# State-space scan: decay sums and their exponentials kept as DRAM rows and read back to all partitions, in place of selector and mask products

## The reference, cut to what matters

```
cum = cumsum(a_c)                            # a = dt * A, along the 128 tokens
seg = cum[i] - cum[j]
decay = exp(where(i >= j, seg, -inf))        # 128 x 128 for each head
cb = C_c @ B_c.T                             # one for a group of 4 heads
y_intra = (cb * decay) @ x_c
y_inter = (C_c @ state) * exp(cum)
new_state = state * exp(cum[-1]) + B_c.T @ (exp(cum[-1] - cum) * x_c)
```

## Time and profile before

| what | value |
|---|---|
| time, median of 3 runs | 1479.23 us (1479.05 to 1479.36) |
| span of the profiled execution | 1476.2 us |
| its own time beside the span | not listed apart; the median of the runs lies 3.0 us above the span |
| PE busy | 98% of the span |
| DVE, ACT, POOL busy | 60%, 42%, 13% |
| PE on the chain of work that ended last | 91% |
| DMA moved | 142.9 MB, mean 97 GB/s |

### The profile page before, as it was taken

One profiled execution on the slowest core, in us unless ns is written; L12 is line 12 of the kernel. 1 busy time (PEld: TensorE's weight loads), 2 busy tenths in 40 slices (PEclk: granted clock), 3 DMA queues, 4 the chain that ended last, 5 costly groups with the idle time before them and its releaser, 6 DMA issues.

```text
span 1476.2 us, 25723 instructions
## 1 busy us (share of the span) xinstructions
PE 1451.7 (98%) x10269; PEld 1154.9 (78%) x10269; DVE 883.7 (60%) x1223; ACT 622.1 (42%) x965; POOL 197.0 (13%) x233
## 2 busy tenths in 40 slices
PE   8999999999999999999999999999999999999897
PEld 4778788787888888788887888888887777777676
DVE  3677677777545765964546443244334876666736
ACT  4664444454555523232334432134323444453534
POOL 0000000000027888820005100000000000000000
PEclk9999999999999999999999999999999999999999
DMA  9432222223245666532332333333332311211111
GB/s 318 130 86 72 72 73 74 79 63 83 75 128 145 167 174 173 169 101 86 100 101 73 100 100 101 100 86 100 100 100 72 86 45 45 60 44 42 51 42 57
DMA packets 263980, 142.89 MB, mean 97 GB/s; under 512 B 4869, under 2 KB 261946, under 8 KB 263866
## 3 DMA queue, kind: packets, MB, share of 16 engines
q1 hardware_dynamic: 263866, 141.26, 33.6%
HBM read 139.14 MB, written 2.10 MB: 96 GB/s over the span
## 4 chain that ended last, share of the span: by engine, by line
PE 91%; DVE 4%; ACT 2%; SPq 1%; issue 1%; DMA 1%; DVEq 0%; ACTq 0%
PE PS L594 25%; PE PS L596 24%; PE PS L595 24%; PE PS L815 1%; PE PS L799 1%; PE PS L1088 1%; PE PS L1104 1%; DMA wm<-in_w_mod_dram 1%; DVE Hl L1860 1%; PE PS L779 1%; PE PS L820 1%; SPq L413 1%; PE PS L1096 1%; PE PS L1044 1%; PE PS L985 1%
## 5 line engine op out<-in xcount | busy, mean ns | idle before, releaser
L594 PE MATMUL PS<-Hh,whi 128*128 128x512 f32 x1226 | 502.7, 410 | 2.7 <-DVE Hl L1860 2.3
L596 PE MATMUL PS<-Hh,wlo 128*128 128x512 f32 x1226 | 478.8, 391 | 0.0
L595 PE MATMUL PS<-Hl,whi 128*128 128x512 f32 x1226 | 478.7, 390 | 0.0
L1848 DVE TENSOR_TENSOR wlo<-raw,whi 128x1024 fp32r<-128x1024 f32 (+1 forms) x211 | 283.4, 1343 | 113.5 <-ACT whi L1283 112.7
L1283 ACT ACTIVATE whi<-raw 128x1024 fp32r<-128x1024 f32 (+1 forms) x211 | 221.7, 1051 | 151.5 <-PE PS L596 146.5
L594 PEld LDWEIGHTS PS<-Hh,whi 128*128 128x128 f32 x1226 | 230.5, 188 | 65.9 <-issue 19.4
L596 PEld LDWEIGHTS PS<-Hh,wlo 128*128 128x128 f32 x1226 | 230.6, 188 | 50.0 <-issue 0.2
L595 PEld LDWEIGHTS PS<-Hl,whi 128*128 128x128 f32 x1226 | 231.1, 188 | 46.5 <-issue 4.8
L492 POOL TENSOR_TENSOR mbuf<-mbuf,cact 128x1024 f32<-128x1024 f32 x32 | 62.2, 1944 | 438.8 <-DMA mbuf<-in_w_mod_dram 438.8
L594 PE MATMUL PS<-YBh,whi 128*128 128x512 f32 x256 | 99.6, 389 | 0.0
L595 PE MATMUL PS<-YBl,whi 128*128 128x512 f32 x256 | 99.6, 389 | 0.0
(11 more groups left out here) (426 smaller groups left out, 1822.3 us busy)
## 6 DMA issues: line engine op xcount, KB each, us to landing
raw<-in_w_in_dram SPq DMA_DIRECT2D x106, 512.0 KB, 4.0
raw<-in_w_ff_dram SPq DMA_DIRECT2D x64, 512.0 KB, 4.1
mbuf<-in_w_mod_dram SPq DMA_DIRECT2D x32, 512.0 KB, 3.9
wm<-in_w_mod_dram SPq DMA_DIRECT2D x8, 1024.0 KB, 10.8
raw<-in_w_branch_ssm_dram SPq DMA_DIRECT2D x16, 512.0 KB, 4.0
raw<-in_w_out_dram SPq DMA_DIRECT2D x10, 512.0 KB, 4.1
raw<-in_w_branch_gm_dram SPq DMA_DIRECT2D x8, 512.0 KB, 4.1
raw<-in_w_out_dram SPq DMA_DIRECT2D x6, 448.0 KB, 3.9
```

What stands on the lines that cost most here:

```text
L594: pe.matmul(bank[:, :], whi[s][:, k, :], xh[:, kk, :], start=kk == 0, stop=False)
L595: pe.matmul(bank[:, :], whi[s][:, k, :], xl[:, kk, :], start=False, stop=False)
L596: last = pe.matmul(bank[:, :], wlo[s][:, k, :], xh[:, kk, :], start=False, stop=t == end - 1 and k == (order or range(kt))[-1])
L1848: v.tensor_tensor(wlo[s][:, 0:kt, :], raw[s][:, 0:kt, :], whi[s][:, 0:kt, :].bitcast(F32), ALU.subtract).then_inc(s_wlo, 1)
```

## The change

The kernel after computes the sums once as fp32 rows on 32 partitions (`er`: sums, `et`: their exponentials). SP writes both to DRAM (`rows_out`), waits for them, and for each chunk issues a transfer that reads one row of 4 heads x 128 tokens back to all 128 partitions (`load_rows`: `crow`, and for c > 0 `erow`), two buffers of each. The mask and selector products, their constants, and the splitting into bf16 parts go. ACT makes Relu(own sum - row) for four heads and one Exp over 512 columns with scale -1; DVE multiplies the 128 x 128 block C B with `triu` (in `inputs`) in place of the mask, and `receivers` reads `erow` in place of bank 6.

```diff
+    erow = region(60, *((f"erow{i}", [P, T]) for i in range(2)))
+    cum_rows, exp_rows = (nc.dram_tensor(name, (NC, 32 * P), F32, kind="Internal").ap() for name in ("cum_rows", "exp_rows"))
...
+        def rows_out():
+            sp.wait_ge(s_dta, 8)
+            for to, rows in ((cum_rows, er), (exp_rows, et)):
+                sp.dma_start(to.rearrange("c (h t) -> h c t", t=P),
+                             rows[0:32, :].rearrange("p (c t) -> p c t", c=NC)).then_inc(s_rows, 16)
+            sp.wait_ge(s_rows, 32)
+
+        def load_rows(n):
+            g, c = divmod(n, NC)
+            e = 3 * g + c - 1
+            at = slice(g * T, (g + 1) * T)
+            if n >= 2:
+                sp.wait_ge(s_dec, n - 1)
+            sp.dma_start(crow[n % 2][:, :], cum_rows[c:c + 1, at].to_broadcast([P, T])).then_inc(s_crow[n % 2], 16)
+            if c > 0:
+                if e >= 2:
+                    sp.wait_ge(s_ch, e - 1)
+                sp.dma_start(erow[e % 2][:, :], exp_rows[c:c + 1, at].to_broadcast([P, T])).then_inc(s_erow[e % 2], 16)
+
+        rows_after = {}
+        for n in range(30):
+            g, c = divmod(n, NC)
+            rows_after[(tile0[("cv", 4 * g + 4)] if g < 7 else tile0[("v", 0)]) + 5 + (10 * c + 10) // 8] = n + 2
...
             load(t)
+            if t == tile0[("z", 0)] + 5:
+                rows_out()
+                load_rows(0)
+                load_rows(1)
+            if t in rows_after:
+                load_rows(rows_after[t])
...
                     for c in range(NC):
-                        for i in range(3):
-                            ms = pe.matmul(BK[6][32 * i:32 * i + 32, c * 128:(c + 1) * 128], AA[:, c * 32:(c + 1) * 32],
-                                           triu[:, :], start=True, stop=True)
+                        ms = pe.matmul(BK[6][0:32, c * 128:(c + 1) * 128], AA[:, c * 32:(c + 1) * 32], triu[:, :],
+                                       start=True, stop=True)
...
-            def decay_sums(c):
...
-            def exp_rows(c):
...
                     if s == 10 * c + 2:
-                        decay_sums(c)
                         turned(c)
-                        if c > 0:
-                            exp_rows(c)
...
-                    act.activation(cumb[0:96, :], BK[6][0:96, :], ACTF.Copy).then_inc(s_dta, 1)
+                    act.activation(er[0:32, :], BK[6][0:32, :], ACTF.Copy).then_inc(s_dta, 1)
                 if s == 19:
-                    act.activation(et[0:96, :], BK[6][0:96, :], ACTF.Exp).then_inc(s_dta, 1)
+                    act.activation(et[0:32, :], BK[6][0:32, :], ACTF.Exp).then_inc(s_dta, 1)
...
                 if i == 0:
-                    act.wait_ge(s_seg, n + 1)
+                    act.wait_ge(s_crow[n % 2], 16 * (n // 2 + 2))
...
-                    e = act.activation(dec[n % 2][:, h * 128:(h + 1) * 128], BK[3][:, h * 128:(h + 1) * 128], ACTF.Exp,
-                                       bias=NCU[:, cc:cc + 1])
+                    act.activation(dec[n % 2][:, h * 128:(h + 1) * 128], crow[n % 2][:, h * 128:(h + 1) * 128],
+                                   ACTF.Relu, bias=CU[:, cc:cc + 1], scale=-1.0).then_inc(s_lag, 1)
                 if i == 1:
-                    e.then_inc(s_dec, 1)
+                    act.wait_ge(s_lag, 4 * n + 4)
+                    act.activation(dec[n % 2][:, :], dec[n % 2][:, :], ACTF.Exp, scale=-1.0).then_inc(s_dec, 1)
...
                 v.tensor_tensor(h4(xdt[n % 2][:, :]), h4(xn[n % 2][:, 0:256]), colh(DT, c), ALU.mult).then_inc(s_xdt, 1)
+                own(v.tensor_tensor(xn[n % 2][:, 384:512], xn[n % 2][:, 384:512], triu[:, :], ALU.mult))
...
             def receivers(c):
-                v.wait_ge(s_eb, 3 * g + c)
-                v.tensor_tensor(h4(ch[n % 2][:, :]), h4(BK[6][:, :]),
+                v.wait_ge(s_erow[e % 2], 16 * (e // 2 + 2))
+                v.tensor_tensor(h4(ch[n % 2][:, :]), h4(erow[e % 2][:, :]),
```

More of the change, by code:

```diff
@@ L18 @@
 KT = 8
-NEG = -1.0e30
 DONE = object()
@@ L55, in build_program @@
     identb = sb("identb", [P, P], BF16)
-    maskb = sb("maskb", [P, P], BF16)
-    sel3 = sb("sel3", [96, 32], BF16)
     selc = sb("selc", [P, 2])
@@ L91, in build_program @@
         *((f"xr{i}", [P, T + 3]) for i in range(2)),
-        ("er", [P, T]), ("et", [P, T]), ("midb", [P, T], BF16), ("cumb", [P, T], BF16), ("expb", [P, T], BF16))
+        ("er", [P, T]), ("et", [P, T]), *((f"crow{i}", [P, T]) for i in range(2)))
     dec, xn, ch, yv, xdt, xw, state, xr = (stemps[2 * i:2 * i + 2] for i in range(8))
-    er, et, midb, cumb, expb = stemps[16:21]
+    er, et, *crow = stemps[16:20]
+    erow = region(60, *((f"erow{i}", [P, T]) for i in range(2)))
+    cum_rows, exp_rows = (nc.dram_tensor(name, (NC, 32 * P), F32, kind="Internal").ap() for name in ("cum_rows", "exp_rows"))
     sqb = region(82, *((f"sqb{i}", [P, T]) for i in range(8)))
@@ L228, in build_program @@
     s_mraw = s_wm[4:6]
+    s_crow, s_erow = s_wm[0:2], s_wm[2:4]
     s_whi, s_wlo, s_tile = sem("s_whi"), sem("s_wlo"), sem("s_tile")
@@ L237, in build_program @@
     s_cx, s_ca, s_c3, s_ct, s_F = sem("s_cx"), sem("s_ca"), sem("s_taps"), sem("s_tanh"), sem("s_F")
-    s_seg, s_tr, s_eb, s_sn, s_yi = sem("s_seg"), sem("s_tr"), sem("s_exp_rows"), sem("s_state_new"), sem("s_yi")
+    s_rows, s_lag, s_tr, s_sn, s_yi = sem("s_rows_out"), sem("s_lag"), sem("s_tr"), sem("s_state_new"), sem("s_yi")
     s_dec, s_xn, s_xdt, s_xw, s_M, s_ch, s_st = (sem(n) for n in ("s_dec", "s_xn", "s_xdt", "s_xw", "s_M", "s_ch", "s_st"))
@@ L484, in pool_program @@
                                ALU.add).then_inc(s_const, 1)
-        pool.wait_ge(s_const, 12)
+        pool.wait_ge(s_const, 7)
         pool.tensor_tensor(selc[:, 0:1], selc[:, 0:1], selc[:, 1:2], ALU.add).then_inc(s_const, 1)
@@ L658, in pe_program @@
         pe.wait_ge(s_cact, 1)
-        pe.wait_ge(s_const, 13)
+        pe.wait_ge(s_const, 8)
         pe.wait_ge(s_xt0, 5)
@@ L775, in turned @@
                 pe.wait_ge(s_F, 6 * g + 4)
-                if n > 0:
-                    pe.wait_ge(s_xn, n)
+                pe.wait_ge(s_xn, n) if n > 0 else pe.wait_ge(s_pc, 5)
                 for j in range(3):
@@ L1347, in dt_steps @@
                     act.activation(EL, BK[7][:, 128:256], ACTF.Exp).then_inc(s_dta, 1)
-                    act.activation(cumb[0:96, :], BK[6][0:96, :], ACTF.Copy).then_inc(s_dta, 1)
+                    act.activation(er[0:32, :], BK[6][0:32, :], ACTF.Copy).then_inc(s_dta, 1)
                 if s == 19:
-                    act.activation(et[0:96, :], BK[6][0:96, :], ACTF.Exp).then_inc(s_dta, 1)
-                    act.wait_ge(s_dta, 8)
-                    act.activation(expb[0:96, :], et[0:96, :], ACTF.Copy).then_inc(s_dta, 1)
+                    act.activation(et[0:32, :], BK[6][0:32, :], ACTF.Exp).then_inc(s_dta, 1)
                 if s == 21:
@@ L1355, in dt_steps @@
                     act.activation(WE, WE, ACTF.Exp).then_inc(s_dta, 1)
[L1356 to L1369, removed]
                 yield
@@ L1965, in dt_steps @@
                     v.wait_ge(s_dta, 6)
-                    v.tensor_scalar(NCU, BK[7][:, 0:128], -1.0, None, ALU.mult).then_inc(s_dtv, 1)
+                    v.tensor_copy(CU, BK[7][:, 0:128]).then_inc(s_dtv, 1)
                     v.wait_ge(s_dtv, 6)
-                    v.tensor_tensor(WE, BK[7][:, 128:256], NCU, ALU.add).then_inc(s_dtv, 1)
-                if s == 21:
+                    v.tensor_tensor(WE, BK[7][:, 128:256], CU, ALU.subtract).then_inc(s_dtv, 1)
+                if s == 24:
                     v.wait_ge(s_dta, 9)
[L1971 to L1975, removed]
-                    v.tensor_tensor(WE, WE, DT, ALU.mult).then_inc(s_dtv, 1)
[L1977 to L1984, removed]
+                    v.tensor_tensor(WE, WE, DT, ALU.mult).then_inc(s_dtv, 1)
                 yield
@@ L2039, in inputs @@
                 v.tensor_tensor(h4(xdt[n % 2][:, :]), h4(xn[n % 2][:, 0:256]), colh(DT, c), ALU.mult).then_inc(s_xdt, 1)
+                own(v.tensor_tensor(xn[n % 2][:, 384:512], xn[n % 2][:, 384:512], triu[:, :], ALU.mult))
             def inputs_end(c):
                 n = 4 * g + c
-                v.wait_ge(s_dtv, 10)
+                v.wait_ge(s_dtv, 8)
                 v.tensor_tensor(h4(xw[n % 2][:, :]), h4(xn[n % 2][:, 0:256]), colh(WE, c), ALU.mult).then_inc(s_xw, 1)
@@ L2049, in decayed @@
                 v.wait_ge(s_dec, n + 1)
+                v.wait_ge(s_dve, nown)
                 v.tensor_tensor(h4(d[:, :]), h4(d[:, :]), xn[n % 2][:, 384:512].unsqueeze(1).to_broadcast([P, 4, P]),
```

## The result

The kernel after takes 1460.82 us (1459.2 to 1461.0, 4 runs) against 1479.3 us (1479.05 to 1479.47, 4 runs): ratio 0.9866, 95% interval 0.9852 to 0.988, 1.3% faster. The forecast was 1459.6. The experiments ran on three chips, each beside runs of the kernel before, so between them I compare lengths of the scan and not medians. On one of them the same kernel took 1457.05 us (1456.78 to 1461.02) against 1479.44 (1477.87 to 1483.31), ratio 0.9854 (0.9834 to 0.9874).

What follows compares the result with a forecast made beforehand. PE was taken to bound the scan, without gaps. Span 1476.2 - 20.4 (products removed) + 0.3 (neighbours) + 0.5 (first rows) = 1456.6, plus 3.0 offset: 1459.6 us; own range 1457 to 1463, 8 in 10 1456.5 to 1467.

Steps and rivals of the forecast that it cites:

- What bounds the kernel: Scan: PE without gaps sets the time; a removed product saves its distance to the next; together 20.4 us.
- The fp32 switch: Scan, `turned` directly behind a tile product, waits ahead of an fp32 weight load: 1.5 us lost, bounds 0.8 to 3.2.
- neighbours: Products beside the removed ones: 1.2 us gained on tile products after `exp_rows`, 1.5 lost at `turned`; net 0.3 lost.
- The sums in one block: Sums on three blocks of partitions become one: 24 records in 1.04 us become eight, 0.7 us saved.
- The first rows: Chunk 0 of group 0: first `crow` lands near 82, PE's output 0 is delayed; 0.5 us lost, bounds 0 and 3.
- The cover: Chunk 2, ACT's start to PE's output: added ACT and DVE work is free; of 4.2 us slack 2.6 stay.
- The more-ACT rival: Less gain: ACT falls behind beside the `v` tiles, 4 to 10 us with late first rows, 1463.5 to 1470; chance 0.13.
- The slower rival: Row transfers fill the transfer engines in the scan; above 4.3 us each they pace it, 1527 at 5.5; chance 0.04.
- The range: Whole run: own range 1457 to 1463 us, term bounds 0.7 better, 2.9 plus 2.5 worse; 8 in 10: 1456.5 to 1467.
- The offset: Whole run: the median lies 3.0 us above the profiled span of 1476.2 us, taken as constant.

Runs made afterwards that it cites:

- the first profile: First profiled execution of the unchanged kernel after: span 1459.6 us; its second profile had a span of 1455.7 us.

## Why the prediction was right

- What bounds the kernel: right. PE sets the scan, and a product costs its distance in the chain. Put back, the mask and sum products cost 13.9 (forecast 14.2), the exponentials' 6.3 (5.5 plus 1.2 for the next tile product).
- The fp32 switch, priced at 1.5 us with bounds 0.8 and 3.2: nothing. A group fell by 2.61; products and neighbours give 4 x 0.445 + 3 x (0.23 + 0.05) = 2.62.
- The sums in one block, 0.7 us: nothing, since the three blocks had run beside each other.
- The first rows, 0.5 us lost: nothing. The forecast put the writes of `rows_out` behind the load issued at 73.39 us; SP issued them at 71.85, the first row at 75.78, and ACT began at 79.73, not 82. The first `dec` ended at 83.65 in place of 86.1 to 86.6, 2.5 us before PE's output. ACT waited 1.3 us at most for a row. PE also lost its 0.3 us wait for DVE before the first transposes; that the copies that went are the reason is not shown.
- The cover: right that there is enough, wrong in where it lies. The forecast counted from DVE's `dec` to the output, in chunk 2, and had 2.6 us left. The output waits for `ch`, which DVE makes behind `dec`, already in the kernel before (232.78 + 0.68, 2.95 us before the output at 236.41, where the forecast had 4.2). In the kernel after `dec` leaves more than forecast in chunk 2, 3.5 us, but `ch` leaves 2.3 there and 1.6 in chunk 3. That this was still enough is partly luck.
- The more-ACT rival did not happen: beside the `v` tiles `ch` ends 2.0 us or more before the outputs. No table load stands before a Relu, in the groups or beside Gelu; beside the `v` tiles ACT has 7 loads, not the 9 that the forecast expected to stay.
- The slower rival, transfers that fill the engines: twice the rows are still free. It needed 4.3 us of all engines for each row; seven more rows raised the share from 0.46 to 0.74 of 41 us, which by my estimate is 1.6 us each. What would have made the kernel slower is the place of the issue, one tile later.
- The range: its own terms allowed 0.7 us better for the neighbours and 0.5 for the first rows, 1.2 in sum and not 0.7.
- The offset: the sum used 3.0 us between span and median. Every later profile has 1.2 us between an execution's span and its time (1459.6 and 1460.85; 1458.4 and 1459.66). By that, the profiled execution of before took about 1477.4 us, an estimate, and was faster than the median. That is 1.8 us too many in the sum.
- The clock: the first profile lost 2.7 + 1.9 us in stretches of half clock, without a changed instruction there. The mean granted clock of the four timed runs was 0.990 three times and 0.993 once, against 0.997 for the profiled run that had neither loss, which suggests that the median contains such stretches too. Sum by its own time: -21.2 - 0.2 + 2.7 + 0.2 + 1.9 = -16.6, 1476.2 to 1459.6.

So the 1.2 us by which the first median missed is made of errors of both signs: 1.6 us more gained in the scan than forecast, 1.8 too much for the offset, and 4.6 of clock in that execution the other way. What is right is the mechanism in the scan; that the total came out within 1.2 us is luck.

## What to carry to other kernels

Where one engine has no gap, price what leaves its stream by the distance in the chain, but check whether the products run beside each other before dividing a group's time by its records. Work moved to other engines and to transfers is free only up to the slack of the chain they feed: lengthen that chain on purpose, and delay the transfer, to learn how much there is, and read from the trace which operand of the consumer is ready last. Where the bounding engine falls idle, count the clock as well: late rows cost 41.6 us of waiting, and 19.5 us by which the products took longer at a lower granted clock. Cut two profiles at common instructions before reading a difference of spans: here two untouched stages held 4.6 us that another execution of the same program did not have.

## What was not expected of the hardware

- A 2 KB row of DRAM read to all 128 partitions (256 KB) lands in 4.8 us behind a 512 KB weight tile, which itself lands in 3.9: below the 6 to 7 us from adding the two. With twice the rows the median is 6.6.
- Twelve fp32 products into three blocks of 32 partitions (24 records) take as long as four into one (8 records): 1.04 us before and 1.00 when put back, 0.99 after.
- Executions of one program differ by 4 to 5 us (1456.78 to 1461.02 for the kernel after on one chip): at the start (66.3 to 69.2 us to the scan in the variants), and by where stretches of half clock fall.
